# A norm's scaled rows and the gated products kept in place in PSUM instead of in SBUF

## What is computed

```python
def rmsnorm(x, g):
    y = x * rsqrt(mean(x * x) + EPS)
    return y * g

def ffn_sublayer(h, m, g, w13, w2, base):
    hn = modulate(rms_norm(h, g), m[base], m[base + 1])   # h * (1 + scale) + shift
    return h + 0.5 * m[base + 2] * swiglu_2(hn, w13, w2)
```

## Time and profile before

| what | value |
|---|---|
| median of three runs | 2643.8 us (2641.78 to 2644.22) |
| the profiled execution, its own time | 2636.59 us |
| its span | 2634.8 us |
| PE matmul busy | 2472.8 us, 94% |
| PE weight loads busy | 2013.5 us, 76% |
| DVE busy | 1703.0 us, 65% |
| ACT busy | 1150.8 us, 44% |
| POOL busy | 1351.7 us, 51% |
| mean granted clock of PE | 0.978 of full speed |
| HBM read | 493.02 MB, 188 GB/s over the span |

### The profile page before, as it was taken

The page is one execution under the profiler, slowest core; times in us unless marked ns, Lnnn a source line. Parts: engine busy times, 40 slices in busy tenths (PEclk is TensorE's granted clock), DMA queues, the critical chain, the costliest instruction groups (busy, mean ns, idle before and its releaser), DMA issues.

```text
span 2634.8 us, 31082 instructions
## 1 busy us (share of the span) xinstructions
PE 2472.8 (94%) x11415; PEld 2013.5 (76%) x11415; DVE 1703.0 (65%) x1912; ACT 1150.8 (44%) x1338; POOL 1351.7 (51%) x691
## 2 busy tenths in 40 slices
PE   7998899999999899999989989989999999997998
PEld 6886667788788677788868868777778878876886
DVE  5776557677766645667787766654677576555554
ACT  4434453443443535344444343344354443444433
POOL 4994120799897212079889959920088088000000
PEclk9999999999999999999999989989999999998999
DMA  7664333666575432477767768744177567553553
GB/s 252 222 226 150 113 104 120 222 226 222 192 230 196 141 125 92 135 253 255 254 206 259 245 192 262 234 144 148 49 231 239 182 224 240 178 174 96 191 186 109
DMA packets 312484, 495.30 MB, mean 188 GB/s; under 512 B 14478, under 2 KB 221610, under 8 KB 312266
## 3 DMA queue, kind: packets, MB, share of 16 engines
q1 hardware_dynamic: 289306, 412.54, 48.4%
q0 software_dynamic: 22800, 80.54, 9.5%
q10 hardware_dynamic: 288, 1.05, 0.1%
HBM read 493.02 MB, written 1.05 MB: 188 GB/s over the span
## 4 chain that ended last, share of the span: by engine, by line
PE 78%; DVE 9%; POOL 6%; ACT 4%; issue 2%; DVEq 1%; ACTq 0%; DMA 0%; SPq 0%; PEldq 0%; PEld 0%; POOLq 0%
PE ps L780 74%; POOL arena L712 2%; DVE wlo L453 2%; POOL arena L702 2%; PE ps L1031 2%; ACT whi L440 1%; DVE HTlo L1724 1%; PE ps L909 1%; POOL arena L687 1%; DVEq L372 1%; POOL arena L733 1%; DVE arena L1718 1%; ACT work L1324 0%; ACTq L372 0%; PE ps L902 0%
## 5 line engine op out<-in xcount | busy, mean ns | idle before, releaser
L453 DVE TENSOR_TENSOR wlo<-raw,whi 128x2048 fp32r<-128x2048 f32 (+5 forms) x405 | 1076.9, 2662 | 465.8 <-ACT whi L440 461.1
L780 PE MATMUL ps<-whi,HThi 128*128 128x512 f32 (+3 forms) x2328 | 937.0, 402 | 57.7 <-DVE HTlo L1724 19.2
L440 ACT ACTIVATE whi<-raw 128x2048 fp32r<-128x2048 f32 (+4 forms) x405 | 752.8, 1861 | 385.6 <-PE ps L780 378.3
L780 PE MATMUL ps<-wlo,HThi 128*128 128x512 f32 (+3 forms) x2328 | 915.2, 393 | 0.0
L780 PE MATMUL ps<-whi,HTlo 128*128 128x512 f32 (+3 forms) x2328 | 914.3, 393 | 0.0
L780 PEld LDWEIGHTS ps<-whi,HThi 128*128 128x128 f32 (+1 forms) x2328 | 443.3, 190 | 163.1 <-DVE HTlo L1724 23.1
L780 PEld LDWEIGHTS ps<-wlo,HThi 128*128 128x128 f32 (+1 forms) x2328 | 442.9, 190 | 94.1
L780 PEld LDWEIGHTS ps<-whi,HTlo 128*128 128x128 f32 (+1 forms) x2328 | 443.8, 191 | 84.0
L712 POOL TENSOR_TENSOR arena<-arena 128x1024 f32<-128x1024 f32 (+1 forms) x170 | 500.4, 2943 | 9.7
L702 POOL TENSOR_TENSOR arena<-arena,cond 128x1024 f32<-128x1024 f32 x184 | 451.2, 2458 | 30.8 <-DMA arena<-in_mod_w_dram 23.3
L687 POOL DMA_DIRECT2D arena<-in_mod_w_dram x144 | 114.0, 792 | 439.6 <-DVEq L372 373.7
(11 more groups left out here) (212 smaller groups left out, 1588.8 us busy)
## 6 DMA issues: line engine op xcount, KB each, us to landing
raw<-in_ffn_w_dram SPq DMA_DIRECT2D x330, 512.0 KB, 4.6
raw<-in_w_ffn_gu_dram SPq DMA_DIRECT2D x176, 512.0 KB, 4.8
arena<-in_mod_w_dram POOLq DMA_DIRECT2D x144, 512.0 KB, 4.6
raw<-in_w_ffn_down_dram SPq DMA_DIRECT2D x88, 512.0 KB, 4.4
raw<-in_w_in_dram SPq DMA_DIRECT2D x40, 1024.0 KB, 5.1
raw<-in_even_w_in_dram SPq DMA_DIRECT2D x12, 1024.0 KB, 5.1
raw<-in_conv_w_in_dram SPq DMA_DIRECT2D x12, 1024.0 KB, 5.2
raw<-in_w_out_dram SPq DMA_DIRECT2D x8, 1024.0 KB, 5.1
```

The lines of the kernel that those rows point to most:

```text
L440: i = nc.scalar.activation(whi[0:rows, r, a:b], raw[0:rows, r, a:b], ACT.Copy)
L453: i = nc.vector.tensor_tensor(wlo[0:rows, r, a:b], raw[0:rows, r, a:b], whi[0:rows, r, a:b].bitcast(F32), ALU.subtract)
L780: return nc.tensor.matmul(o, lhsT, rhs, start=first, stop=last)
```

## The change: the rows stay in PSUM

`hf` is no tile of SBUF any more but a name for the two PSUM banks of a block. Gain and shift are written back over the turned rows, and both the copy to `HThi` and the subtraction for `HTlo` read PSUM. In the gated FFNs the gated product is written over y in PSUM, and the addition reads it there; the gated `dense` phases do the same. No semaphore, no wait and no order of instructions is changed, and the count of instructions stays.

```diff
-        hf = arena[:, 2048:4096].rearrange("p (c t) -> p c t", c=DC)
+
+        def hf(b, half):
+            return ps[:, 4 + 2 * b + half, :].rearrange("p (k t) -> p k t", k=4)
@@ norm_block, ACT
-                            i = A(hf[:, k, b * P:(b + 1) * P], ps[:, 4 + 2 * b + half, (k % 4) * P:(k % 4 + 1) * P],
-                                  ACT.Identity, scale=ph["gain"][:, k:k + 1], bias=ph["shift"][:, k:k + 1])
+                            i = A(hf(b, half)[:, k % 4], hf(b, half)[:, k % 4], ACT.Identity, scale=ph["gain"][:, k:k + 1], bias=ph["shift"][:, k:k + 1])
@@
-                    A(HThi[:, 4 * half:4 * half + 4, b * P:(b + 1) * P],
-                      hf[:, 4 * half:4 * half + 4, b * P:(b + 1) * P], ACT.Copy).then_inc(sem("h_hi"), 1)
+                    A(HThi[:, 4 * half:4 * half + 4, b * P:(b + 1) * P], hf(b, half), ACT.Copy).then_inc(sem("h_hi"), 1)
@@ norm_parts, DVE
-                        V.tensor_tensor(hf[:, 4 * half:4 * half + 4, b * P:(b + 1) * P],
-                                        ps[:, 4 + 2 * b + half, :].rearrange("p (k t) -> p k t", k=4),
+                        V.tensor_tensor(hf(b, half), hf(b, half),
@@
-                        i = V.tensor_scalar(hf[:, k, b * P:(b + 1) * P], ps[:, 5 + 2 * b, (k - 4) * P:(k - 3) * P],
-                                            ph["gain"][:, k:k + 1], ph["shift"][:, k:k + 1], ALU.mult, ALU.add)
+                        i = V.tensor_scalar(hf(b, 1)[:, k - 4], hf(b, 1)[:, k - 4], ph["gain"][:, k:k + 1], ph["shift"][:, k:k + 1], ALU.mult, ALU.add)
@@
-                    V.tensor_tensor(HTlo[at], hf[at], HThi[at].bitcast(F32), ALU.subtract).then_inc(sem("h_ready"), 1)
+                    V.tensor_tensor(HTlo[at], hf(b, half), HThi[at].bitcast(F32), ALU.subtract).then_inc(sem("h_ready"), 1)
@@ end of a gated FFN
-                            link(V.tensor_tensor(xn[:, b, :], y, gateB, ALU.mult))
-                            V.tensor_tensor(x[:, b, :], x[:, b, :], xn[:, b, :], ALU.add).then_inc(sem(name), 1)
+                            link(V.tensor_tensor(y, y, gateB, ALU.mult))
+                            V.tensor_tensor(x[:, b, :], y, x[:, b, :], ALU.add).then_inc(sem(name), 1)
@@ gated dense
-                                    gated = work[:, (P2 + b) * 512:(P2 + b + 1) * 512]
-                                    link(V.tensor_tensor(gated, p, gateB[:, n0:n0 + 512], ALU.mult))
-                                    i = V.tensor_tensor(o, o, gated, ALU.add)
+                                    link(V.tensor_tensor(p, p, gateB[:, n0:n0 + 512], ALU.mult))
+                                    i = V.tensor_tensor(o, p, o, ALU.add)
```

## The result

The changed kernel took 2626.7 us in the median of four runs (2623.66 to 2628.83), the kernel before 2642.8 beside it; the ratio is 0.995 [0.9936, 0.9964]. Two later comparisons on the chip gave 0.9959 [0.9945, 0.9973] and 0.9957 [0.9942, 0.9973]. Three of the four runs of before in this comparison are the ones that the prediction started from, so its -16.1 us (2642.8 to 2626.7) doesn't test that start; the later comparisons do. In the two profiled executions, 2636.59 and 2628.83 us, it was -7.8.

The account below looks back on a forecast made before the run. PE's matmuls bound the kernel, partly idle at norms where `HTlo` waits for POOL's SBUF reads. Terms -4.5 - 2.0 - 3.7 + 1.4 + 0.4 = -8.4 us, 2643.8 to 2635.4; range 2630 to 2642.5.

Parts of the forecast that it names:

- `HTlo` takes 0.69 us always: At every norm, the subtraction reading PSUM no longer waits for POOL; its mean was 1049 ns, its longest 3609.
- Fifth, -4.5: Norm ahead of the fifth FFN: PE's waits go; 5.2 us if `wlo` starts before POOL's next instruction, 3.6 otherwise; 4.5 taken.
- Seventh, -2.0: Norm ahead of the seventh FFN: PE's waits of 1.27, 0.50 and 0.27 us go, 2.0 us gained.
- Eighth, -3.7: Norm ahead of the eighth FFN: PE's 2.08 us wait and 1.6 us of lowered clock go; 2.1 if the clock falls.
- Handover, +1.4: From second to third FFN: earlier `wlo` holds up POOL's last additions, so PE starts 1.4 us later.
- Sixth, 0, or 2.3 either way: Sixth FFN: POOL's last sum sets the end, so 0; one turn lost or won against `wlo` is 2.3 us.
- Write-back +0.4: Some 53 DVE instructions on PE's path, written back in PSUM, cost 8 ns more each: 0.4 us lost.
- The slower rival: In-place PSUM writes by DVE take double time per element: 19 us lost, +11 in all, 2655 us; chance 0.07.
- ACT in place, covered: ACT's in-place tiles and half 0 copy at the norms have 0.7 us to spare behind DVE's four: 0.
- Gated products, 0: Gated additions lose an SBUF operand but never waited for POOL, so nothing is gained: 0.
- The given-back rival: DVE's next `wlo` meets the same POOL instruction and PE waits for it instead: -2.2 us in all; chance 0.25.
- the sum is taken from both alike: The terms' sum applies equally to the profiled execution, 2636.6 us, and the runs' median, 2643.8, 7.2 us above it.

Follow-up runs that it names:

- before_again: The kernel before, unedited, run and profiled once more; against itself 0.9997 [0.9984, 1.001], 2637.2 us in the median of 12 runs.
- elsewhere: The changed kernel with norm rows in PSUM only at the nine norms not beside POOL, gated products through SBUF; 1.0001 [0.9987, 1.0014] to the kernel before.
- gate_only: The changed kernel with the norm's rows back through SBUF, only the gated products in PSUM; 1.0004 [0.9992, 1.0015] to the kernel before.
- norm_only: The changed kernel with the gated products back through SBUF, only the norm's rows in PSUM; 0.9957 [0.9942, 0.9971] to the kernel before.
- beside_pool: The changed kernel with norm rows in PSUM only at the five norms beside POOL, gated products through SBUF; 0.9948 [0.9928, 0.9968] to the kernel before.
- after_again2: The changed kernel, unedited, run and profiled a third time; its two repeats took 2626.4 and 2628.3 us.
- after: The changed kernel's first profile, an execution of 2628.83 us; 2626.7 us in the median of four runs.

## Why the prediction was right and wrong

- *`HTlo` takes 0.69 us always*: right, 677 to 693 ns.
- *Fifth, -4.5*: right place and mechanism, mis-sized. It is -5.4 to -5.6, near the 5.2 that was worked out for a tie that is won; against the mean of three profiles of before (+0.6) it is -6.1.
- *Seventh, -2.0*: -1.7, -1.8 and -3.0. The two waits for `HTlo` went, but in the first two of these profiles the one for `wlo` grew (1.04 and 0.89 us for 0.27) where it should have gone.
- *Eighth, -3.7*: right against the profile that it was read from (-3.5 to -4.3). Against three it is -2.4, since before has the wait only in some executions: of the five with `HTlo` in SBUF here, `before_again` and `elsewhere` had none and `gate_only` 1.48 us.
- *Handover, +1.4*: +1.1 to +1.8 against the profile that it was read from, by the mechanism that was forecast. But that was a favourable draw: against the five executions without the change it is some +0.4, less than these differ among themselves.
- *Sixth, 0, or 2.3 either way*: +1.9, -1.2, +1.8, and -1.4 to -1.5 in `norm_only` and `beside_pool`; before has 0, -1.5 and -0.1. So it goes both ways, as was said. DVE still stands for POOL's last sum, 6.42 us for 6.43:

```profile
1707.82 0.45 DVE L1651 STREAM_TRANSPOSE arena<-arena 128x256 f32<-128x256 f32 x1 [6.42 <-POOL work L717]
```

- *Write-back +0.4*: DVE's pays 8 to 10 ns for the 8 assumed. The slower rival (an in-place write at double time per element) is out: 694 ns at 128x512 in place, against 684 to SBUF, is not double.
- *ACT in place, covered*: right, and it was quicker besides.
- *Gated products, 0*: right, 1.0004.
- *The given-back rival* holds for the 0.8 us at the seventh; otherwise not.

The step that failed is "the sum is taken from both alike": the base. The sum was made against 2636.6 and then subtracted from 2643.8, the median of three runs, as if the 7.2 us between them were something that the change leaves alone. By 68 runs the kernel takes 2639.0, 4.8 less. Whether the first three were high by chance is not settled; the medians beside the later comparisons, on four chips, are 2637.9 to 2640.1. From 2639.0 the same sum gives 2630.6, and the range, moved by the same 4.8, is 2625.2 to 2637.7 and holds 2626.7. The remaining 3.1, -11.5 against -8.4, are in the terms. By the means of three profiles each, the fifth gave 1.6 more than its 4.5, and the last mixer and norm 1.3 that the sum had at nothing, while the eighth gave 1.3 less than its 3.7. The rest is what chance gives and takes in places where before and after both vary, and isn't assigned. The range was also built from the change's terms alone, with nothing in it for a kernel whose own executions spread over 17 us.

On the page that I had weighed: the row decided rightly. The Trainium skill (VectorE: DVE Perf Modes, the TRN2 errata) has 58 fixed cycles for an SBUF source and 120 for a PSUM one, an estimated 65 ns more; here the same subtraction takes 690 ns from PSUM and 692 or 693 from SBUF in the median. For the wait itself this case's rows speak: beside POOL 1516 ns with two SBUF operands and 687 with one, and 690 with two and POOL quiet. The Trainium skill (SBUF - State Buffer, "Who interferes with whom") says the same: a VectorE instruction with two SBUF inputs contends with a GpSimd one that reads SBUF, one with at most one SBUF input, outside the two-port modes, doesn't.

## What to carry to other kernels

Look at the longest instruction of a line beside its median: where GpSimd is at work, the excess is a wait that no idle column shows, and moving one of two SBUF operands to PSUM takes it away. What it is worth depends on what stands behind the freed instruction: the weight unit behind the norm gained with it, while at the handover an earlier `wlo` meets POOL's last sum, for which PE waits. And before a forecast is subtracted from a median, see how far the kernel's own runs lie apart.

## What the runs showed that I had not expected

- The spread of this kernel is mostly the order of DVE and POOL. The kernel before runs from 2628.6 to 2645.8 us over 68 runs; with POOL's arithmetic left out, it and its changed form stay within 2605.2 to 2609.6 over 12 runs.
- The wait can be for more than the instruction under way. At the fifth norm the second `HTlo` was due at 1330.3, when POOL was issuing a DMA, and yet ended at 1333.3, after POOL's next product. Where `wlo` came while a product was running it went ahead at the product's end (1344.08, above). But not every instruction that comes during a DMA issue waits. In `after_again2` `wlo` began at the seventh norm at 1923.09, 0.08 us into an issue, and took 2.29 us; in `after` it began at 1924.03, 0.12 us into the issue there, and took 5.28. In `before_again` a `HTlo` began at 2127.93, 0.18 us into one, and took 0.68; there POOL's next product came only at 2129.17. What decides was not found.
- A wait of PE can be followed by eight matmuls at half the clock, 1.6 us more. Such episodes come and go at the same few places from one execution to the next, and where one follows, a wait taken away is worth nearly twice its length (the eighth: 2.08 + 1.6). Not every wait brings one: the 1.48 us in `gate_only` at the same place did not.
